# A two-layer decoder step on one Trainium2 core: the expert layer's query projection in one pass over all 320 tokens, in place of 128 tokens first and 192 behind them

## The reference, cut to what matters

```
def block(tb):                       # tb: 128 tokens
    q = (tb @ wq).reshape(PEER_BLOCK, N_PEER_HEADS, 2, D_KEY_HALF)
    s = jnp.einsum('thpk,hpnk->thpn', q, subkeys).astype(jnp.float32)
    s_top, i_top = lax.top_k(s, TOPK)
    cand = (s_top[:, :, 0, :, None] + s_top[:, :, 1, None, :]).reshape(...)
    cand_idx = (i_top[:, :, 0, :, None] * N_KEYS + i_top[:, :, 1, None, :]).reshape(...)
    best, sel = lax.top_k(cand, TOPK)
    experts = jnp.take_along_axis(cand_idx, sel, axis=-1)
    g = jax.nn.softmax(best, axis=-1).astype(tb.dtype)
    act = jax.nn.gelu(jnp.einsum('td,thkd->thk', tb, u[experts]), approximate=False)
    return jnp.einsum('thk,thkd->td', g * act, v[experts])
```

## Time and profile before

| | |
|---|---|
| median of 3 runs | 2919.91 us (2919.18 to 2921.19) |
| profiled execution | 2910.3 us, its span 2908.5 us |
| PE busy | 2670.3 us (92% of the span) |
| DVE busy | 1443.5 us (50%) |
| DMA | 885.12 MB, mean 304 GB/s |
| the expert part of layer 0 | about 884 to 1705 us of the span |
| the expert part of layer 1 | about 2065 to 2887 us of the span |

### The profile page before, as it was taken

The page is one execution under the profiler, slowest core; times in us unless marked ns, Lnnn a source line. Parts: engine busy times, 40 slices in busy tenths (PEclk is TensorE's granted clock), DMA queues, the critical chain, the costliest instruction groups (busy, mean ns, idle before and its releaser), DMA issues. The chain is left out here.

```text
span 2908.5 us, 40661 instructions
## 1 busy us (share of the span) xinstructions
PE 2670.3 (92%) x16221; PEld 2200.1 (76%) x16221; DVE 1443.5 (50%) x3443; ACT 357.4 (12%) x1030; POOL 674.6 (23%) x679
## 2 busy tenths in 40 slices
PE   7978998669989999999999999998999999999996
PEld 4456446334648999999999967454799999999996
DVE  1322002002125996998555422023499889955553
ACT  2311012001201111111000010011111121100000
POOL 0133500000000332445333200000033334443330
PEclk8688999779999999999999999999999999999998
DMA  4676995999490798999999989469249989999995
GB/s 140 209 256 210 265 348 171 407 400 344 149 358 31 286 373 323 335 353 339 409 409 409 387 307 363 143 248 394 84 189 379 353 309 352 343 394 409 409 409 175
DMA packets 249626, 885.12 MB, mean 304 GB/s; under 512 B 31629, under 2 KB 38957, under 8 KB 238706
## 3 DMA queue, kind: packets, MB, share of 16 engines
q1 hardware_dynamic: 165358, 591.12, 54.9%
q0 software_dynamic: 84080, 291.41, 26.7%
HBM read 863.08 MB, written 109.08 MB: 334 GB/s over the span
## 5 line engine op out<-in xcount | busy, mean ns | idle before, releaser
L2667 PE MATMUL ps<-xT,front 128*128 128x192 f32 x4096 | 689.0, 327 | 10.4 <-issue 6.3
L2667 PEld LDWEIGHTS ps<-xT,front 128*128 128x128 f32 x4096 | 666.6, 191 | 14.5 <-DMA front<-in_peer_uT 6.8
L2693 PE MATMUL ps<-p1e_S,p_qT 128*128 128x192 f32 x2048 | 336.9, 327 | 5.2 <-DMA p_qT<-in_peer_v 5.2
L2693 PE MATMUL ps<-p0e_S,p_qT 128*128 128x192 f32 x2048 | 337.0, 327 | 4.8 <-DMA p_qT<-in_peer_v 4.8
L2693 PEld LDWEIGHTS ps<-p1e_S,p_qT 128*128 128x128 f32 x2048 | 332.4, 190 | 9.3 <-DMA p_qT<-in_peer_v 9.3
L2693 PEld LDWEIGHTS ps<-p0e_S,p_qT 128*128 128x128 f32 x2048 | 332.4, 190 | 9.0 <-DMA p_qT<-in_peer_v 8.9
L2460 DVE CUSTOM_DVE_ANT_0 front<-front,x_tok 128x1024 f32<-128x1024 f32 x256 | 309.8, 1218 | 6.1 <-DMA front<-in_peer_u,p0e_expert 2.3
L2361 POOL DMA_INDIRECT front<-in_peer_u,p1e_expert x128 | 153.4, 1199 | 398.9 <-DVE p1e_dots L2460 207.7
L2361 POOL DMA_INDIRECT front<-in_peer_u,p0e_expert x128 | 153.4, 1198 | 398.6 <-DVE p0e_dots L2460 207.5
L2471 DVE SCALAR_TENSOR_TENSOR h_tok<-front,p0e_dots,h_tok 128x1024 f32<-128x1024 f32 x127 | 163.1, 1285 | 142.9 <-DMA front<-in_peer_v,p0e_expert 136.6
L2471 DVE SCALAR_TENSOR_TENSOR h_tok<-front,p1e_dots,h_tok 128x1024 f32<-128x1024 f32 x127 | 163.1, 1284 | 142.2 <-DMA front<-in_peer_v,p1e_expert 137.6
(11 more groups left out here) (483 smaller groups left out, 3087.7 us busy)
## 6 DMA issues: line engine op xcount, KB each, us to landing
front<-in_peer_uT SPq DMA_DIRECT2D x256, 512.0 KB
p_qT<-in_peer_v SPq DMA_DIRECT2D x256, 512.0 KB
out_swa_sample<-in_cache_swa_w SPq DMA_DIRECT2D x32, 2040.0 KB, 21.6
e_ring<-in_swa_kT SPq DMA_DIRECT2D x16, 1024.0 KB, 9.3
e_arena<-in_swa_v SPq DMA_DIRECT2D x16, 1024.0 KB, 15.2
out_swa_sample<-in_cache_swa_w SPq DMA_DIRECT2D x8, 2016.0 KB, 28.2
e_ring<-in_mla_pages SPq DMA_DIRECT2D x56, 272.0 KB
e_ring<-in_attn_w_in SPq DMA_DIRECT2D x6, 2048.0 KB, 24.5
```

The source lines that it names most:

```text
L2667: mm = pe.matmul(k.ps[:, SB[i % len(SB)], 0:TD], ur[:, i % NU, c, :], k.xT[:, c, D0:T], start=(c == 0), stop=(c == KC - 1))
L2693: mm = pe.matmul(k.ps[:, c // 2, c % 2 * TD:(c % 2 + 1) * TD], vr[:, i % NV, c * P:(c + 1) * P], S[:, i, :], start=False, stop=(i == STEPS ...
```

## The change

`query`, `take_q` and the two loops on PE and ACT lose their second pass: each query block is computed once for all 320 tokens, and copied once. Each of the 16 blocks is then 8 float32 matmuls over 320 columns, where it was 8 over 128 and, in the second pass, 8 over 192. Score 0 to 2 of tile 0 stay behind query blocks 5, 9 and 13; the fourth score of tile 0 (`score(3)`) and the eight of tiles 1 and 2 now stand behind the last query block.

```diff
-            def take_q(b, t0, n):
-                act.wait_ge(q_done, (b if t0 == 0 else CHUNKS * BLOCKS + b) + 1)
-                bank = (b if t0 == 0 else CHUNKS * BLOCKS + b) % QB
-                act.activation(pqT[:, b, t0:t0 + n], k.ps[:, bank, 0:n], ACT.Copy).then_inc(q_taken, 1)
+            def take_q(b):
+                act.wait_ge(q_done, b + 1)
+                act.activation(pqT[:, b, :], k.ps[:, b % QB, 0:T], ACT.Copy).then_inc(q_taken, 1)
...
             for b in range(CHUNKS * BLOCKS):
-                take_q(b, 0, P)
+                take_q(b)
                 if b % BLOCKS == 1 and b > BLOCKS:
                     take_scores(b // BLOCKS - 1)
-            for b in range(CHUNKS * BLOCKS):
-                take_q(b, P, TD)
-                if b == 1:
-                    take_scores(CHUNKS - 1)
-                if b % BLOCKS == 1 and b > BLOCKS:
-                    for i in range(2):
-                        take_scores(CHUNKS + 2 * (b // BLOCKS - 1) + i)
-            for order in range(len(SCORES) - 2, len(SCORES)):
+            for order in range(CHUNKS - 1, len(SCORES)):
                 take_scores(order)
...
-            def query(b, t0, n):
-                done = b if t0 == 0 else CHUNKS * BLOCKS + b
-                if b % BLOCKS == 0 and t0 == 0:
+            def query(b):
+                if b % BLOCKS == 0:
                     pe.wait_ge(k.wq_landed[b // BLOCKS], 16 * (layer + 1))
-                if done >= QB:
-                    pe.wait_ge(q_taken, done - QB + 1)
+                if b >= QB:
+                    pe.wait_ge(q_taken, b - QB + 1)
                 for c in range(KC):
-                    mm = pe.matmul(k.ps[:, done % QB, 0:n], wq[b // BLOCKS][:, c, b % BLOCKS * P:(b % BLOCKS + 1) * P],
-                                   k.xT[:, c, t0:t0 + n], start=(c == 0), stop=(c == KC - 1))
+                    mm = pe.matmul(k.ps[:, b % QB, 0:T], wq[b // BLOCKS][:, c, b % BLOCKS * P:(b % BLOCKS + 1) * P],
+                                   k.xT[:, c, :], start=(c == 0), stop=(c == KC - 1))
                 mm.then_inc(q_done, 1)
...
-                pe.wait_ge(q_taken, (0 if i == 0 else CHUNKS * BLOCKS) + BLOCKS * (c + 1))
+                pe.wait_ge(q_taken, BLOCKS * (c + 1))
```

More of the change, by code:

```diff
@@ L2712, in _ @@
             for b in range(CHUNKS * BLOCKS):
-                query(b, 0, P)
+                query(b)
                 if b % BLOCKS == 1 and b > BLOCKS:
                     score(b // BLOCKS - 1)
[L2716 to L2723, removed]
+            for order in range(CHUNKS - 1, len(SCORES)):
                 score(order)
```

## The result

The changed kernel takes 2947.98 us (median of 4, 2945.39 to 2953.17), the kernel before 2920.55 us beside it (median of 4): ratio 1.0089 with a 95% interval of 1.0074 to 1.0103 (the ratios here and below are as recorded; the quotient of the two medians is 1.0094). By the medians it is slower by 27 us; 33 were forecast. The profiled execution took 2945.39 us, 35.1 us more than that of before, where the sum gave 32.8.

The account below looks back on a forecast made before the run. PE was taken as the bound, with DVE's chain deciding the gates before the turned keys. Shifts of 15.5 and 13.9 us plus 3.4 us of clock gave 32.8 us over 2919.9: 2953 us, 8-in-10 range 2942 to 2962, own range 2944 to 2959.

Parts of the forecast that it names:

- DVE's start: DVE's fourth piece of tile 0, which follows score(3), starts 35.8 us later in each layer.
- DVE's chain: DVE's work from tile 0's last scores to the gates: unchanged; at best layer 0's 2.3 us of waits go away.
- Rival 3: Gathers are starved and DVE waits for rows: 3 to 5 us a layer more, 2961 us; chance 0.10.
- The cover: Time in hand at the gates absorbs 20.3 us (layer 0) and 21.9 us (layer 1), leaving shifts of 15.5 and 13.9 us.
- PE's wait: New wait of PE before the turned keys, ended by DVE: about 17 us in layer 0, 15 in layer 1.
- my own bound of 3 us: Sign at the turned keys: the prediction is wrong if PE's wait differs from forecast by more than 3 us.
- The clock: PE runs at a reduced clock behind its new wait: 1.7 us lost a layer, bounds 0 and 2.4.
- The stretch behind: From the keys to each layer's end: as long as before, except for the clock.
- rival 2: PE regains the loss in its 28.1 us of waits for blocks of `v`; at the extreme 2924.6 us; chance 0.05.
- From the profiled execution to the median: Whole kernel: the median's 9.6 us above the profiled execution carried over, taking 2943.1 us to 2952.7 us.
- Rival 1: Delay of score(3) covered at the gates if below 20.3 us: 2916.9 us, within 0.2%; chance 0.04.

Follow-up runs that it names:

- groups 1 and 3: Two sets of follow-up runs, each on its own chip; the kernel before, unchanged, took 2923.93 us in group 1 and 2918.33 us in group 3.
- group 2: Set of follow-up runs on another chip, where the kernel before took 2878.78 us and was not profiled.
- late_score: Kernel before with its two query passes kept, only the scores ordered as in the change: 2951.64 us, ratio 1.0087.
- wide8: Kernel before with query blocks 0 to 7 merged into one pass over 320 columns, blocks 8 to 15 in two passes: 2923.87 us, ratio 0.9999.
- after_warm_late: Changed kernel, with PE doing 8 matmuls of zeros towards the end of its wait before the turned keys: 2943.17 us, ratio 1.0094.
- before_again: Kernel before, unchanged, run once more: 2923.93 us, ratio 0.9994.
- after_again: Changed kernel, unchanged, run once more on the same chip as before_again: 2949.82 us, ratio 1.0082.
- before_c: Kernel before, unchanged, run once more as the reference of group 3: 2918.33 us, ratio 1.0004.
- paced_c: Kernel before with gathers 2 to 6 of tile 0 issued behind dense steps 0 to 4, not in one burst: 2909.09 us, ratio 0.9975.
- after_warm: Changed kernel, with PE doing 14 matmuls of zeros ahead of its wait before the turned keys: 2924.78 us, ratio 1.0150.

## Why the prediction was right

**DVE's start.** Forecast 35.8 us later, measured 37.0 in both layers. The extra us is the start of the stage: 913.36 - 884.96 = 28.4 us for 96 records that cost 25.9, so 2.5 us and not the 1.49 of the earlier trace rows. The wide kernel's first windows have the clock at 0.50 and then 0.78. Before, it was 0.56 and full in the next 4 us:

```profile
888.00:892.00 4.00, 4.00 (x38) 1.00 0.65 260
```

**DVE's chain.** Forecast as unchanged, with the end of today's 2.3 us of waits as the lower bound. Fourth piece to gates took 961.62 to 1169.27 us, 207.7 us, against 924.30 to 1134.19, 209.9 us: the lower bound was the right value in layer 0. In layer 1 it took 2368.45 - 2159.64 = 208.8 us against 2313.80 - 2105.28 = 208.5 us. Rival 3, starved gathers, did not show in the result or in groups 1 and 3 (DVE's waits at the row products are 0 to 1.3 us, 2.6 once, in the changed kernel). In group 2 they are 4.3 to 5.1 us a layer in the two versions of the changed kernel; that the change brought them there is not shown, since the kernel before has no profile on that chip.

**The cover.** Forecast shifts of the keys 15.5 and 13.9 us, 29.4 in sum; measured 14.1 and 15.0, 29.0 in sum. This is the term that carries the prediction. `late_score` and `wide8` show it from both sides: past the cover, without wide blocks, the whole loss; just inside the cover, with eight of them, none. That the sum comes so close is in part luck, since three misses offset each other: DVE's start 1.2 us later than forecast in each layer, its chain 2.2 us shorter in layer 0, and a cover 0.4 us larger in each layer. The 0.25 us that I deducted for the handing over, an estimate, should not have been deducted: where PE waits, it starts 1170.87 - 1169.27 = 1.60 us behind the start of L2448, so in the kernel before it could have started at 1151.26 + 1.60 = 1152.86 us, and had 1156.47 - 1152.86 = 3.6 us in hand. The cover was 20.7 and 22.3 us. With it the shifts come out as measured: 37.0 us, less the 2.2 us by which DVE's chain is shorter, less 20.7, is 14.1 us in layer 0; 37.0 + 0.3 - 22.3 is 15.0 us in layer 1.

**PE's wait.** Forecast 17 and 15 us, measured 12.0 and 11.5, and by my own bound of 3 us that was wrong. In layer 0 the 5 us are 1.5 us by which the gates came earlier than forecast, and 3.5 us by which PE came later. In layer 1 the gates came 1.1 us later than forecast and PE 5.0 us. PE started step 0 near where I put it (84.9 us behind the first query, forecast 86), but then waited for blocks of `u` and for issue, 5.1 us in layer 0 and 6.4 in layer 1, where it was 1.9 us for `u` behind step 0 in layer 0 of the kernel before. I had kept the 3.18 us ahead of step 0 as a fixed part of the way; it goes with the gathers and moves behind step 0 with them. It cost nothing, since DVE decides there.

**The clock.** Forecast 1.7 us a layer with 2.4 as the upper bound, measured 2.8 and 2.2 from the keys to the first spread; layer 0 is beyond the bound. The mechanism is shown by `after_warm_late`, the size was too small: the 2.0 us after the longest pause were nearer than the value after the short ones. Two windows tell why: behind the wait the clock is at 0.50 for 4.1 us and still at 0.79 in the 4 us after, and I had counted one stretch of 3.4 to 4 us.

**The stretch behind.** Forecast unchanged; spread to end is 1.0 and 0.6 us longer. Nothing came back in the values, rival 2 is out. The three terms make up the profiled pair: 29.0 us of shift, 5.0 of clock and 1.5 behind, 35.6 us before rounding, where the forecast had 29.4, 3.4 and 0.

**From the profiled execution to the median.** The sum fits the profiled pair (32.8 against 35.1) better than the medians (27.4). The step that failed is carrying the 9.6 us between the execution read and the median over unchanged. The execution that I read had the shortest way to the keys of all profiles of that kernel. What other executions lose there, up to 5 us a layer, counts in full in the kernel before and is hidden behind the wait in the changed one: `before_again` against `after_again` is 14.4 + 10.3 = 24.7 us over the two layers, and their medians lie 25.9 us apart. That this makes up the whole gap between 35 and 27 is argued from these few profiles, not shown. The forecast median of 2953 us against 2947.98 is thus a sum 2.3 us too small and a carried difference 7 us too large. By its own terms the forecast's range starts at 2919.9 + 29.4 - 4 = 2945.3 us and not at 2944; nothing hangs on it.

Rival 1, the delay covered, failed at its own point of decision: 37 us are beyond 20.3, and beyond the 20.7 that it was.

## What to carry to other kernels

Merging two passes over the same weights saved little on TensorE here, since the time goes with the columns (an estimated 1.7 us a layer), and it delayed the last result of the first pass by nearly all of the second. Before merging, find who waits for that result and how much time that engine has in hand where it next meets the bottleneck; the loss is the delay less this cover, plus the clock behind the new wait. Read the cover from more than one execution: DVE's idle time at the gates alone was 17.1 to 23.4 us in three profiles of the kernel before, and it can be spent on something that pays, such as pacing a burst of gathers.

## What the runs showed of the hardware that was not expected

In the kernel before, a burst of seven indirect gathers of 512 KB (3.7 MB, issued at 1.3 us intervals) goes with a stall of PE ahead of step 0: 3.18 and 3.16 us (`before`), 4.67 and 6.79 us (`before_again`), 3.20 and 3.17 us (`before_c`), 6 to 14 us behind the first gather. In `wide8`, where the gathers start in the middle of the steps, it is 3.61 us with two small gaps, 11 to 20 us behind the first. One gather per 2.6 us took the stall ahead of step 0 away in `paced_c`; single waits for `u` of up to 1.5 us were left. On the chip of group 2 the same burst, started among the steps, left PE waiting for blocks of `u` and for issue no more than 2.1 us in all between step 0 and the keys; whether the kernel before stalls ahead of step 0 there is not known.

Zeros multiplied during a wait of PE kept the clock when they lay at its end, and not when they lay at its start: 9 us of zeros followed by 13.8 us of idle time left it at 0.50, 6.9 us of zeros directly ahead of the work had it at 1.00.

The same kernel took 2879 us on one chip and 2918 to 2924 us on the others. In the profiles of group 2 the first query of layer 0 comes at 855 to 858 us, in all others at 884 to 888 us. In the changed kernel's expert part the waits are PE's for blocks of `u` on the latter chips (4.3 to 6.4 us a layer, with issue) and DVE's for rows on the former (4.3 to 5.1 us). The loss by the change was 0.8% to 1.0% on the latter; on the former `after_warm`, the changed kernel with its zeros, lost 1.5%.
